# Two-layer hybrid trunk, SEQ 256, D 2048: the MLP up-projection with the weights as the stationary operand

## The reference, cut to what matters

```python
def squared_relu_mlp(u, w1, w2):
    hdn = jnp.square(jax.nn.relu(jnp.einsum("bsd,df->bsf", u, w1)))
    return jnp.einsum("bsf,fd->bsd", hdn, w2)
...
    for i in range(DEPTH):               # DEPTH = 2
        ...
        h = h + m                        # m: the layer's token mixer
        h = h + squared_relu_mlp(rmsnorm(h, norm_mlp[i]), mlp_w1[i], mlp_w2[i])
        h = h + per_layer_embedding(h, p[i], norm_ple[i], ple_w_proj[i], ple_w_gate[i])
    return rmsnorm(h, norm_final)
```

## Time and profile before

| | |
|---|---|
| median of 3 runs | 2361.03 us (2360.18 to 2361.15) |
| the profiled execution's own time | 2361.07 us |
| span of its instructions | 2359.3 us |
| mean granted TensorE clock | 0.996 |
| PE busy | 2327.6 us, 99% |
| PE weight loads (PEld) busy | 1932.1 us, 82% |
| DVE busy | 1381.5 us, 59% |
| ACT busy | 993.7 us, 42% |
| DMA | 431.55 MB, mean 183 GB/s |

### The profile page before, as it was taken

One profiled execution on the slowest core, in us unless ns is written; L12 is line 12 of the kernel. 1 busy time (PEld: TensorE's weight loads), 2 busy tenths in 40 slices (PEclk: granted clock), 3 DMA queues, 4 the chain that ended last, 5 costly groups with the idle time before them and its releaser, 6 DMA issues.

```text
span 2359.3 us, 29531 instructions
## 1 busy us (share of the span) xinstructions
PE 2327.6 (99%) x10490; PEld 1932.1 (82%) x10490; DVE 1381.5 (59%) x1709; ACT 993.7 (42%) x1120; POOL 1.6 (0%) x9
## 2 busy tenths in 40 slices
PE   8999999999999999999999999999999999999996
PEld 6888678888888888888888888888888888888885
DVE  5999955555555555555656565555555555555555
ACT  1000445434444444455644444544344344344554
POOL 0000000000000000000000000000000000000000
PEclk9999999999999999999999999999999999999998
DMA  9444155555555555555555555555555555555552
GB/s 299 152 155 157 57 196 178 179 202 190 178 198 193 178 196 196 178 178 192 190 188 189 187 193 180 178 188 190 194 182 190 195 180 193 196 178 196 175 199 107
DMA packets 231278, 431.55 MB, mean 183 GB/s; under 512 B 7180, under 2 KB 40460, under 8 KB 230412
## 3 DMA queue, kind: packets, MB, share of 16 engines
q1 hardware_dynamic: 230448, 428.90, 53.9%
q10 hardware_dynamic: 632, 0.89, 0.1%
q0 software_dynamic: 144, 1.05, 0.1%
HBM read 428.70 MB, written 2.10 MB: 183 GB/s over the span
## 4 chain that ended last, share of the span: by engine, by line
PE 86%; issue 13%; DVE 0%; DMA 0%; ACT 0%; DVEq 0%; POOL 0%; ACTq 0%; POOLq 0%
PE acc L347 28%; PE acc L349 28%; PE acc L348 28%; PE tp L337 2%; DMA work<-in_cf_b_pw 0%; DVE raw L1029 0%; DVE work L723 0%; ACT pT L498 0%; ACT L555 0%; DVE res L769 0%; DVE work L764 0%; DVE wlo L705 0%; DVEq L163 0%; ACT work L510 0%; ACT h L517 0%
## 5 line engine op out<-in xcount | busy, mean ns | idle before, releaser
L705 DVE TENSOR_TENSOR wlo<-raw,whi 128x1024 fp32r<-128x1024 f32 x736 | 890.9, 1223 | 707.5 <-ACT whi L487 697.4
L487 ACT ACTIVATE whi<-raw 128x1024 fp32r<-128x1024 f32 x736 | 768.7, 1057 | 730.2 <-PE acc L349 727.1
L347 PE MATMUL acc<-whi,b_hi 128*128 128x512 f32 x1664 | 651.7, 392 | 1.9 <-DVE wlo L705 1.9
L349 PE MATMUL acc<-whi,b_lo 128*128 128x512 f32 x1664 | 648.5, 390 | 0.0
L348 PE MATMUL acc<-wlo,b_hi 128*128 128x512 f32 x1664 | 648.2, 390 | 0.0
L347 PE MATMUL acc<-whi,a_hi 128*128 128x512 f32 x1280 | 500.4, 391 | 0.0
L349 PE MATMUL acc<-whi,a_lo 128*128 128x512 f32 x1280 | 498.3, 389 | 0.0
L348 PE MATMUL acc<-wlo,a_hi 128*128 128x512 f32 x1280 | 498.2, 389 | 0.0
L347 PEld LDWEIGHTS acc<-whi,b_hi 128*128 128x128 f32 x1664 | 312.9, 188 | 67.3 <-issue 2.5
L349 PEld LDWEIGHTS acc<-whi,b_lo 128*128 128x128 f32 x1664 | 312.7, 188 | 65.2
L348 PEld LDWEIGHTS acc<-wlo,b_hi 128*128 128x128 f32 x1664 | 313.0, 188 | 64.1 <-issue 0.2
(11 more groups left out here) (94 smaller groups left out, 586.3 us busy)
## 6 DMA issues: line engine op xcount, KB each, us to landing
raw<-in_mlp_w SPq DMA_DIRECT2D x256, 1024.0 KB, 5.0
raw<-in_sc_w_in SPq DMA_DIRECT2D x48, 1024.0 KB, 5.0
raw<-in_cf_w_pw SPq DMA_DIRECT2D x64, 512.0 KB, 8.6
raw<-in_ple_w_gate SPq DMA_DIRECT2D x32, 1024.0 KB, 5.0
raw<-in_cf_w_pw SPq DMA_DIRECT2D x16, 1024.0 KB, 5.0
raw<-in_sc_w_out SPq DMA_DIRECT2D x16, 1024.0 KB, 5.0
wproj<-in_ple_w_proj SPq DMA_DIRECT2D x2, 2048.0 KB, 13.9
h<-in_x SPq DMA_DIRECT2D x4, 512.0 KB, 9.3
```

What stands on the lines that cost most here:

```text
L347: nc.tensor.matmul(o, xhi[:, k, s], hi, start=first and c == 0, stop=False)
L349: mm = nc.tensor.matmul(o, xlo[:, k, s], hi, start=False, stop=last and c == 1)
L487: nc.scalar.activation(whi[:, e % SLOTS, :, :], raw[:, e // 2, 2 * (e % 2):2 * (e % 2) + 2, :], ACT.Copy).then_inc(hi_ready, 1)
L705: nc.vector.tensor_tensor(wlo[:, e % SLOTS, :, :], raw[:, e // 2, 2 * (e % 2):2 * (e % 2) + 2, :], whi[:, e % SLOTS, :, :].bitcast(F32), A ...
```

## The change

The up-projection of the MLP, and nothing else, swaps the roles of its operands. The weights become the stationary operand (128 x 128, `whi` or `wlo`), the transposed activations stream through (128 x 256, all tokens at once), and the result has hidden channels on the partitions and 256 tokens in half a bank. For 512 hidden channels that is four groups f, two to a bank. A half then has 2 chunks x 4 groups x 3 matmuls = 24 matmuls of 256 columns. A result of kind "hidden" is not transposed any more: ACT and DVE make hi and lo from `res`, after their fifth half, and a new semaphore `hid_ready` takes the place of `tp_free` for the down unit.

A token's factor r can no longer be applied to partitions, so relu and square are computed without it, and r squared is applied to the result of the down-projection (max(r z, 0)^2 = r^2 max(z, 0)^2 for r > 0). For this norm DVE makes 1 / (mean square + eps), without a root. The down-projection's result is taken out of PSUM by two instructions of 128 x 512.

```diff
-    HID = dict(T=1, t=1, xh=1)
+    HID = dict(t=1, xh=1, hd=1)
...
+        hidden = res[:, :, :].rearrange("p m (c n) -> p (m c) n", n=2 * P)
...
+            def hidden_half(b, e, pair, xin, first, last):
+                pe.wait_ge(lo_ready, HALVES * b + e + 1)
+                xhi, xlo = xin
+                for c in range(2):
+                    k = 2 * e + c
+                    for f in range(4):
+                        o = acc[:, bass.ds(2 * pair + f // 2, 1), f % 2 * 2 * P:(f % 2 + 1) * 2 * P]
+                        s = slice(f * P, (f + 1) * P)
+                        hi, lo = whi[:, e % SLOTS, c, s], wlo[:, e % SLOTS, c, s]
+                        nc.tensor.matmul(o, hi, xhi[:, k, :], start=first and c == 0 and f % 2 == 0, stop=False)
+                        nc.tensor.matmul(o, hi, xlo[:, k, :], start=False, stop=False)
+                        mm = nc.tensor.matmul(o, lo, xhi[:, k, :], start=False, stop=last and c == 1 and f % 2 == 1)
+                mm.then_inc(half_used, 1)
+
+            def hidden_block(b, a, pair, xin, pre=None, ready=None):
+                pe.wait_ge(acc_free, a - 1)
+                for e in range(HALVES):
+                    if ready and e % 2 == 0:
+                        pe.wait_ge(ready[0], ready[1] + e // 2 + 1)
+                    hidden_half(b, e, pair, xin, e == 0, e == HALVES - 1)
+                    if e == 3 and pre is not None:
+                        pe.wait_ge(res_ready, pre[1] + 1)
+                        pe.wait_ge(tp_free, pre[0])
+                        transpose_group((c, m, res[:, m, c * P:(c + 1) * P])
+                                        for c in range(4) for m in range(2))
+
+            def hidden_unit(unit, xin, ready, before):
+                pre = (before.T, before.t) if before.transposed else None
+                hidden_block(unit.b, unit.a, 0, xin, pre, ready)
+                with pe.Fori(1, BLOCKS) as j:
+                    hidden_block(unit.b + j, unit.a + j, j % 2, xin)
...
-                multiply_unit(up[0], X[u], ready, before)
+                hidden_unit(up[0], X[u], ready, before)
                 with pe.Fori(0, GROUPS - 1) as g:
                     w2, w1 = down[0].shifted(by, g), up[1].shifted(by, g)
-                    multiply_unit(w2, X[hid], (tp_free, up[0].shifted(by, g).T),
-                                  Result(up[0].shifted(by, g), BLOCKS - 1))
-                    multiply_unit(w1, X[u], None, Result(w2, BLOCKS - 1))
-                multiply_unit(down[-1], X[hid], (tp_free, up[-1].T), Result(up[-1], BLOCKS - 1))
+                    multiply_unit(w2, X[hid], (hid_ready, up[0].shifted(by, g).hd))
+                    hidden_unit(w1, X[u], None, Result(w2, BLOCKS - 1))
+                multiply_unit(down[-1], X[hid], (hid_ready, up[-1].hd))
...
                 if r.kind == "hidden":                                # ACT, process
                     act.wait_ge(acc_free, r.a + 1)
                     act.wait_ge(tp_done, r.T)
+                    act.wait_ge(hid_ready, r.hd)
                     nc.scalar.activation(res[:, :, :], zb, ACT.Square).then_inc(res_ready, 1)
...
+            def hidden_hi(r, dst):                                    # ACT, after its fifth half
+                act.wait_ge(res_ready, r.t + 1)
+                nc.scalar.activation(dst[0][:, bass.ds(4 * r.j, 4), :], hidden, ACT.Copy).then_inc(xhi_ready, 1)
...
                 if r.kind == "hidden":                                # DVE, process
                     dve.wait_ge(res_ready, r.t)
-                    for m in range(2):
-                        last = nc.vector.tensor_scalar(zb[:, m:m + 1, :], pair_half(r.pair, m),
-                                                       rinv[:, m:m + 1], 0.0, ALU.mult, ALU.max)
-                    last.then_inc(acc_free, 1)
+                    nc.vector.tensor_scalar(zb, both, 0.0, None, ALU.max).then_inc(acc_free, 1)
                     return
                 if r.kind == "add":
                     dve.wait_ge(ss_ready, r.s)
-                    nc.vector.tensor_tensor(here, both, here, ALU.add).then_inc(acc_free, 1)
+                    for m in range(2):
+                        last = nc.vector.scalar_tensor_tensor(h[:, m:m + 1, cols(r.j)], pair_half(r.pair, m), rinv[:, m:m + 1],
+                                                              h[:, m:m + 1, cols(r.j)], ALU.mult, ALU.add)
+                    last.then_inc(acc_free, 1)
...
+                if r.kind == "mlp_out":        # the same two instructions, into res
...
+                if n == NORM_MLP:                                     # DVE, norm
+                    steps.mark(nc.vector.tensor_scalar(mean[:, :], rinv[:, :], 1.0 / D, EPS, ALU.mult, ALU.add))
+                    steps.wait()
+                    steps.mark(nc.vector.reciprocal(rinv[:, :], mean[:, :]))
+                    steps.wait()
+                    return
                 inverse_root(n, rinv[:, :], mean[:, :], rinv[:, :], root[:, :])
...
+            def hidden_lo(r, dst):                                    # DVE, after its fifth half
+                dve.wait_ge(xhi_ready, r.xh + 1)
+                nc.vector.tensor_tensor(dst[1][:, bass.ds(4 * r.j, 4), :], hidden,
+                                        dst[0][:, bass.ds(4 * r.j, 4), :].bitcast(F32),
+                                        ALU.subtract).then_inc(hid_ready, 1)
```

More of the change, by code:

```diff
@@ L31 @@
 SLOTS = 4
-FIELDS = ("b", "a", "T", "t", "xh", "s", "sg")
+FIELDS = ("b", "a", "T", "t", "xh", "s", "sg", "hd")
 class Place:
     def __init__(self, n):
-        self.b, self.a, self.T, self.t, self.xh, self.s, self.sg = (n[f] for f in FIELDS)
+        self.b, self.a, self.T, self.t, self.xh, self.s, self.sg, self.hd = (n[f] for f in FIELDS)
     def counts(self):
-        return dict(zip(FIELDS, (self.b, self.a, self.T, self.t, self.xh, self.s, self.sg)))
+        return dict(zip(FIELDS, (self.b, self.a, self.T, self.t, self.xh, self.s, self.sg, self.hd)))
 class Unit(Place):
@@ L119, in trunk @@
     ROW_LOADS = 10
-    at = dict(b=1, a=HALVES, T=BLOCKS, t=0, xh=UNITS, s=BLOCKS, sg=0)
+    at = dict(b=1, a=HALVES, T=BLOCKS, t=0, xh=UNITS, s=BLOCKS, sg=0, hd=0)
     def place(kind, per, blocks=BLOCKS):
@@ L154, in trunk @@
     gate.append(place("gate_last", dict(t=1, s=1, sg=1)))
-    NORM_CONV, NORM_MLP, NORM_PLE, NORM_WIN, NORM_FINAL = 1, (2, 5), (3, 6), 4, 7
+    NORM_CONV, NORM_PLE, NORM_WIN, NORM_FINAL = 1, (2, 4), 3, 5
+    NORM_MLP = -1
     def distance(u, v):
@@ L241, in trunk @@
         tp_done, tp_free = sem("tp_done"), sem("tp_free")
-        xhi_ready, y_ready = sem("xhi_ready"), sem("y_ready")
+        xhi_ready, y_ready, hid_ready = sem("xhi_ready"), sem("y_ready"), sem("hid_ready")
         ss_ready, junk_written = sem("ss_ready"), sem("junk_written")
@@ L561, in after @@
                         operand_hi(r.T, r.j, dst, gain)
-                    if new_norm is not None:
+                    if new_norm is not None and new_norm != NORM_MLP:
                         take_root(new_norm)
@@ L567, in between @@
                         keep(r)
+                    if e == 4 and r.kind == "hidden":
+                        hidden_hi(r, dst)
                 run(b, lambda: process(r), after, between=between)
@@ L579, in run_mlp @@
                 by = distance(up[0], up[1])
-                run_unit(up[0], hid, None, prev, X[u], ROW_MLP + layer, NORM_MLP[layer])
+                run_unit(up[0], hid, None, prev, X[u], ROW_MLP + layer, NORM_MLP)
                 with act.Fori(0, GROUPS - 1) as g:
@@ L751, in process @@
                 dve.wait_ge(ss_ready, r.s)
-                nc.vector.tensor_tensor(res[:, :, :], both, here, ALU.add).then_inc(acc_free, 1)
+                if r.kind == "mlp_out":
+                    for m in range(2):
+                        last = nc.vector.scalar_tensor_tensor(res[:, m:m + 1, :], pair_half(r.pair, m), rinv[:, m:m + 1],
+                                                              h[:, m:m + 1, cols(r.j)], ALU.mult, ALU.add)
+                    last.then_inc(acc_free, 1)
+                else:
+                    nc.vector.tensor_tensor(res[:, :, :], both, here, ALU.add).then_inc(acc_free, 1)
                 dve.wait_ge(acc_free, r.a + 1)
@@ L827, in between @@
                         add_gated(r)
+                    if e == 4 and r.kind == "hidden":
+                        hidden_lo(r, dst)
                 run(b, lambda: process(r), after, between)
```

## The result

| | before | after |
|---|---|---|
| median of 5 runs | 2361.15 us | 2373.99 us (2373.09 to 2374.05) |
| ratio, 95% interval | | 1.0054, 1.0041 to 1.0067 |
| profiled execution | 2361.07 us | 2373.47 us |
| its span | 2359.3 us | 2371.7 us |

The forecast was 2339, faster; the time is 13 us above the kernel before. It is that of the prediction's first rival (2373: all 13.3 ns are a cost of each matmul).

A forecast was written before the change was run, and what follows sets the result against it. The prediction took PE to bound the kernel, its time the sum of what it issues: -29.0 us (transposes) + 7.1 (slower matmuls) = -21.9, so 2361 - 21.9 = 2339 us, with a range of 2328 to 2376.

The forecast's parts named there:

- the prediction's first rival: Up-projection matmuls: all 13.3 ns are a cost of each matmul, giving 120.0 ns, 11.9 us lost, 2373 us; chance 33%.
- The transposes: On PE's path: 32 results no longer transposed, 0.907 us each, saving 29.0 us.
- the new semaphore: Handover from up to down unit through hid_ready: waits met in time, with 9 us of slack, costed at nothing.
- 7.0 was worked out: Down unit's first block: last quarter of its operand ready 7.0 us after the start, wanted after 16.3 us.
- Weight loads fit in: Up-projection: 3072 more loads, 0.11 us apart, fit beside matmuls of 114.5 ns, costed at nothing.
- the sign for their pace: If loads set the pace (9%, 2393 us): PEld without idle time in up units and starts over 120 ns apart.
- The break-even of 118.1 ns: Up-projection block: 192 matmuls of 256 columns equal the old 22.667 us at 118.1 ns each.
- both main cases: Up-projection loss by the column (43%, 2339 us, or 2332 if all of it) or fixed for each matmul (33%, 2373 us).
- one term: Slower up-projection matmuls: 114.5 ns each, 21.98 us a block against 21.76 without transposes, +7.1 us over 32 blocks.
- "If so, half the columns cost half of it": Up-projection matmuls: 10.9 ns of loss halve at 256 columns, so 106.7 + 2.4 + 10.9 / 2 = 114.5 ns.

The follow-up runs named there:

- experiment 2: The changed kernel with the up-projection matmuls of the kernel before (512 columns, activations stationary) and still no transposes; 2332.14 us.
- Experiments 1: The kernel before, with each 512-column matmul of the up-projection split into two of 256 columns, transposes kept; 2401.04 us.
- 3: The kernel before, with the up-projection's matmuls cut to 384 of 512 columns; 2198.99 us.
- 4: The kernel before, with 64 instead of 128 stationary columns in four of six up-projection matmuls; 2368.45 us.
- 5: The changed kernel with the 24 matmuls of a half reordered so that none adds to the region the one before it wrote; 2374.23 us.
- experiment 6: The kernel before, with the up-projection's matmuls cut to 128 of 512 columns; 2178.99 us.
- experiments 7: The changed kernel with hi x hi and hi x lo streamed as one 512-column matmul, alternating with 256-column ones; 2362.77 us, ratio 1.0006 to the kernel before.
- 8: As experiments 7, but with the activations' hi and lo side by side, so the 512 streamed columns are one contiguous piece; 2360.35 us.
- experiments 9: As experiments 7, but each half runs its eight 512-column matmuls first, then its eight of 256; 2353.79 us, ratio 0.9968 to the kernel before.
- 10: As experiments 9, but every second half runs its 256-column matmuls first; 2352.03 us, ratio 0.9958 to the kernel before.

## Why the prediction was wrong

**Right:** PE is the bound, and the time is the sum of its blocks. The transposes are worth 29.0 us (2 x 14.51 in the chain of experiment 2). DVE, ACT, SP and the new semaphore cost nothing that shows: PE has no new wait inside an MLP. The operand is there 7.3 us into the down unit, where 7.0 was worked out. Weight loads fit in. Half of the sign for their pace did come true, for PEld has no idle time left in an up unit (80.00 us busy from 560 to 640, and 66.49 before); but its records overlap, 0.19 us long and 0.12 apart, and the loads' own pace is 112 ns. The break-even of 118.1 ns holds. The range held the time because it was drawn around both main cases.

**Wrong:** one term, and with it the sign. "If so, half the columns cost half of it" took 10.9 of the 13.3 ns as a cost by the column. Experiments 1 and 3 show that all 13.3 belong to the matmul: 120.0, 173.3 and 226.7 ns for 256, 384 and 512 columns. With 120.0 the prediction's own sum reads -29.0 + 32 x (23.04 - 21.76) = +12.0, a time of 2373; measured were 2374.0.

**Where the reasoning slipped:** I had two facts, that the extra time lies inside the record and that it is gone at the lower clock, and read them as a stream that is too slow all along. A stall that occurs once in a matmul, and does not show at half the clock, fits both as well. The rows held one size of rounded matmul only, so the slope was a guess. The nearest rows on size, float32 operands at 128, 256 and 512 columns, all showed a cost for each matmul (2.3, 2.1 and 2.3 ns, rounded up to 2.4 in the prediction, which moves nothing). Had they weighed more, the two main cases would have changed places.

**The rule of the Trainium skill.** For 256 columns the formula of the Trainium skill ("TensorE: Matmul & The Clock Gate", Back-to-back issue gap), which it gives for isolated matmuls, makes an estimate of 109.2 ns; the trace has 120.0 for rounded operands in a stream, each with a load of its own. The form of it, columns by the clock plus a constant, fits them too, with 13.3 ns as the constant.

**Open:** what in the hardware takes the 13.3 ns. It is not the load's length (4), not two matmuls in a row that add to one region (5), not the orientation (1). Every matmul in these kernels has a weight load of its own, so no run tells a cost of the matmul from a cost of changing the weights. Of the 12.4 us between the two spans the MLPs of the two layers account for 12.0; the rest is less than runs of one kernel differ by.

## What to carry to other kernels

Cost a matmul as columns plus a constant for its kind of operands, and take the constant from the pace of at least two lengths before halving one: at 13.3 ns, splitting 512 columns in two costs 5.9%, which here was more than the transposes it saved. When a change of orientation leaves short matmuls, look for two with the same stationary operand and stream them as one. Then keep equal lengths together: in runs of equal matmuls the constant held every time, where lengths alternated it held in some units and not in most.

## What the runs showed of the hardware

- A matmul of rounded operands (float32r) takes its columns at 2.4 GHz plus 13.3 ns: 120.0, 173.3 and 226.7 ns at 256, 384 and 512 columns (experiments 1 and 3, and the kernel before).
- Weight loads of 128 columns of such operands follow each other every 112 ns at the full clock and every 214 ns at 1.2 GHz (experiment 6). From 112 and 13.3 ns I estimate that at the full clock they are the bound under about 240 columns; between 128 and 256 nothing was run.
- After a change of length the pace takes some matmuls to settle. Alternating 512 and 256 columns cost 6 ns a pair in most units and nothing in some (experiments 7, 8); two changes a half cost 0.02 us a half, and one change half of that (experiments 9, 10).
- Eight transposes cost 0.907 us among matmuls of 512 columns and 0.87 among those of 256 (experiments 1, 2).
- Shorter weight loads made the matmuls beside them no faster, and mixing loads of 64 and 128 columns made them 2 ns slower on average (experiment 4).
